# Attention of the first network: heads in pairs on the two halves of the TensorE array, the mask added in PSUM, another spread of the convolution's taps

## The reference

```python
h = modulate(rmsnorm(x, norm1_g[l]), sh1, sc1)
p = h @ w_in[l]                      # GLU 2x512 | q k v 3x512 | two gates 2x1024
q = rope_2d(q, ...); k = rope_2d(k, ...)
y_conv = conv_branch(...)            # GLU, depthwise convolution of 31 taps, layernorm, silu, @ w_conv_out
# neighbourhood attention, 8 heads of 64; all 4 grid rows, a window of 16 of 64 columns, and the context
s_win = einsum("bhqd,bhiqjd->bhqij", q_r, k_win) * scale + rpb[...]
s_ctx = einsum("bhqd,bhcd->bhqc", q_r, k_ctx) * scale
p = softmax(concatenate([s_win, s_ctx]))
y = p_win @ v_win + p_ctx @ v_ctx
# first layer only: the context attends to itself, with softmax(q_c k_c * scale) v_c
x = x + g1 * ((sigmoid(p_gate) * [y_conv, y_attn @ w_na_out]) @ w_out)
x = x + g2 * conv_ffn(modulate(rmsnorm(x), sh2, sc2))
```

## Time and profile before

| | us |
|---|---|
| median of 3 runs (2118.94 to 2122.93) | 2121.02 |
| the profiled execution | 2119.22 |
| its span, first to last instruction | 2117.4 |

### The profile page before, as it was taken

One profiled execution on the slowest core, in us unless ns is written; L12 is line 12 of the kernel. 1 busy time (PEld: TensorE's weight loads), 2 busy tenths in 40 slices (PEclk: granted clock), 3 DMA queues, 4 the chain that ended last, 5 costly groups with the idle time before them and its releaser, 6 DMA issues.

```text
span 2117.4 us, 34274 instructions
## 1 busy us (share of the span) xinstructions
PE 2014.3 (95%) x12568; PEld 1697.1 (80%) x12568; DVE 1022.9 (48%) x1916; ACT 889.8 (42%) x1505; POOL 1185.1 (56%) x904
## 2 busy tenths in 40 slices
PE   5999999999999999999999999899899999989997
PEld 3666666777888788887789998787799987769997
DVE  3167876726343322587666732466542034546402
ACT  3222433424333322525546644446454343545533
POOL 1332333343544555454487986564588856629885
PEclk8999999999999999999999999999899999989999
DMA  9799221233623232344344575333355544315663
GB/s 390 273 343 326 65 60 60 75 117 75 162 89 99 90 100 89 95 125 115 95 160 142 186 222 171 108 112 102 95 177 179 178 141 153 109 59 180 185 185 107
DMA packets 115686, 306.55 MB, mean 145 GB/s; under 512 B 29672, under 2 KB 44392, under 8 KB 115316
## 3 DMA queue, kind: packets, MB, share of 16 engines
q1 hardware_dynamic: 112664, 298.06, 43.9%
q10 hardware_dynamic: 2908, 6.90, 1.7%
HBM read 300.19 MB, written 8.06 MB: 146 GB/s over the span
## 4 chain that ended last, share of the span: by engine, by line
issue 42%; POOL 37%; PE 18%; DVE 1%; POOLq 0%; ACT 0%; DMA 0%; ACTq 0%
POOL w_lo L600 37%; PE bank L1082 5%; PE bank L1084 4%; PE bank L1083 4%; PE bank L1483 1%; PE bank L1484 1%; PE bank L1485 1%; DVE nb L1725 0%; PE bank L1659 0%; DVE u_lo L1733 0%; PE bank L1512 0%; POOLq L596 0%; PE bank L1699 0%; PE bank L1675 0%; PE bank L1605 0%
## 5 line engine op out<-in xcount | busy, mean ns | idle before, releaser
L600 POOL TENSOR_TENSOR w_lo<-raw,w_hi 128x512 fp32r<-128x512 f32 x884 | 1167.5, 1346 | 911.1 <-ACT w_hi L641 910.6
L641 ACT ACTIVATE w_hi<-raw 128x1024 fp32r<-128x1024 f32 x442 | 466.3, 1056 | 321.2 <-PE bank L1084 250.4
L1082 PE MATMUL bank<-h_hi,w_hi 128*128 128x512 f32 (+1 forms) x1216 | 423.4, 348 | 8.2 <-POOL w_lo L600 4.3
L1083 PE MATMUL bank<-h_lo,w_hi 128*128 128x512 f32 (+1 forms) x1216 | 415.3, 341 | 0.0
L1084 PE MATMUL bank<-h_hi,w_lo 128*128 128x512 f32 (+1 forms) x1216 | 415.2, 341 | 0.0
L1082 PEld LDWEIGHTS bank<-h_hi,w_hi 128*128 128x128 f32 x1216 | 229.0, 188 | 64.8 <-issue 27.6
L1082 PE MATMUL bank<-u_hi,w_hi 128*128 128x272 f32 (+1 forms) x880 | 255.0, 290 | 9.5 <-POOL w_lo L600 4.2
L1084 PEld LDWEIGHTS bank<-h_hi,w_lo 128*128 128x128 f32 x1216 | 229.1, 188 | 29.3
L1083 PEld LDWEIGHTS bank<-h_lo,w_hi 128*128 128x128 f32 x1216 | 229.2, 188 | 28.2 <-issue 0.2
L1083 PE MATMUL bank<-u_lo,w_hi 128*128 128x272 f32 (+1 forms) x880 | 251.7, 286 | 0.0
L1084 PE MATMUL bank<-u_hi,w_lo 128*128 128x272 f32 (+1 forms) x880 | 251.5, 286 | 0.0
(11 more groups left out here) (289 smaller groups left out, 3494.0 us busy)
## 6 DMA issues: line engine op xcount, KB each, us to landing
raw<-in_wstream SPq DMA_DIRECT2D x442, 512.0 KB, 3.6
ada_raw<-in_wada SPq DMA_DIRECT2D x96, 512.0 KB, 7.0
biash<-rpb_by_offset SPq DMA_DIRECT2D x64, 64.0 KB, 3.5
rpb_by_offset<-in_rpb SPq DMA_DIRECT2D x16, 224.0 KB
bias_by_distance<-vec ACTq DMA_DIRECT2D x1, 3264.0 KB
bias<-bias_by_distance SPq DMA_DIRECT2D x2, 1632.0 KB, 8.7
X<-in_x_in ACTq DMA_DIRECT2D x1, 2048.0 KB, 11.9
bias<-bias_by_distance SPq DMA_DIRECT2D x2, 864.0 KB, 6.7
```

The source lines that it names most:

```text
L600: i = pool.tensor_tensor(w_lo[:, s, part], raw[:, s, part], w_hi[:, s, part].bitcast(F32), ALU.subtract)
L641: act.activation(w_hi[:, s, :], raw[:, s, :], ACT.Copy).then_inc(sem("w_hi_ready"), 1)
L1082: pe.matmul(o, hi, a_hi, start=start, stop=False)
L1083: pe.matmul(o, hi, a_lo, start=False, stop=False)
```

## The change

- Heads are handled as pairs (2p, 2p+1). `scores_x` takes a list of heads: for pairs 1 to 3 the scores of both heads are issued together, half t=0 of both and then t=1 of both; heads 0 and 1 stay apart.
- `values` takes a pair: for each block of keys the even head's product and then the odd one's, into the two column halves of bank 7; `pt_x` and `pt_c` exist twice. Rounding and rest of the values are made once for a pair, on 128 partitions.
- `turn` becomes `turn_x` and `turn_c`, separate steps; the context scores of the even head follow the pair's scores, those of the odd head its transposes.
- The mask is no longer added to the bias: for each half it is added to the scores in PSUM behind the bias.
- VectorE walks a list of its own, `VECTOR1_PLAN`, with the taps as steps: in the first layer 3, 7 and 4 in a pair, 6 beside each v slab; in the second 2, 5 and 3, and 10.
- Bias loads of heads 2 and up stand one (even) or two (odd) slabs earlier on the queue.

```diff
-        pt_x = at("pt_x", [4, 256], F32, work + 6144)
-        pt_c = at("pt_c", [2, 256], F32, work + 10240)
+        pt_x = [at(f"pt_x{u}", [4, 256], F32, o) for u, o in enumerate((work + 6144, nb_at))]
+        pt_c = [at(f"pt_c{u}", [2, 256], F32, o) for u, o in enumerate((work + 10240, nb_at + 4096))]
...
+            V_ = [("V", p - 1)] * (p > 0)
+            if p:
+                L1_PLAN += [("Sx", e, o), ("Sc", e), ("gate", 4 * p)] + V_
+            else:
+                L1_PLAN += [("gate", 0), ("Sx", o)]
+            L1_PLAN += [("gate", 4 * p + 1), ("Tx", e), ("Tc", e), ("gate", 4 * p + 2), ("Tx", o), ("Sc", o)]
+            L1_PLAN += [("mean", 0)] * last + [("gate", 4 * p + 3), ("Tc", o)]
+            VECTOR1_PLAN += [("Sx", e, o), ("Sc", e)] if p else [("Sx", o)]
+            VECTOR1_PLAN += [("tap", 2), ("Tx", e), ("Tc", e)] + V_
+            VECTOR1_PLAN += [("tap", 5 if not last else 0), ("Tx", o), ("Sc", o), ("tap", 3 if not last else 0)]
+            VECTOR1_PLAN += [("mean", 0)] * last + [("Tc", o)]
...
-        TAPS_QK, TAPS_V, TAPS_HEAD = 7, 4, 4
+        TAPS_QK, TAPS_V = 7, (6, 10)
...
-                    loads(gate + 2 * h + 2)
+                    loads(gate + 2 * h + (1, 0)[h % 2])
...
+            def scores_x(layer, heads):
                 pe.wait_ge(*after("rope_out", (layer, 2 * QC - 1)))
                 for t in range(2):
+                    for h in heads:
+                        claim(sx_bank(h, t))
+                for t in range(2):
+                    for h in heads:
+                        r = slice((h % 2) * HD, (h % 2) * HD + HD)
+                        b = sx_bank(h, t)
+                        pe.matmul(bank[b][:, :], qT[r, h // 2, t * P:(t + 1) * P], kT[r, h // 2, :], start=True, stop=True)\
+                            .then_inc(*done("attn_score", (layer, h, t)))
...
+            def values(layer, p):
                 claim(7)
...
                 for k in range(4):
...
+                    for u in range(2):
+                        h = 2 * p + u
+                        mm = pe.matmul(aux[3][u * HD:(u + 1) * HD, 0:SEQ], V[:, k, h * HD:(h + 1) * HD], pt_x[u][:, k, :],
+                                       start=k == 0, stop=k == 3)
...
                     if 0 in units:
                         dve.wait_ge(*after(f"bias_in{h % 2}", (layer, h, 1, 1)))
-
-                        m = win.unsqueeze(1).to_broadcast((P, 8, GRID_W))
-                        tt(bh.rearrange("p t (a b) -> p (t a) b", a=4), bh.rearrange("p t (a b) -> p (t a) b", a=4), m, ALU.add)\
-                            .then_inc(*done("bias_masked", (layer, h)))
-                        dve.wait_ge(*after("bias_masked", (layer, h)))
+                    window = win.unsqueeze(1).to_broadcast((P, 4, GRID_W))
...
                             tt(ps[:, 0:SEQ], ps[:, 0:SEQ], bh[:, u, :], ALU.add).then_inc(*done("attn_added", (layer, h, u)))
+                            near = ps[:, 0:SEQ].rearrange("p (a b) -> p a b", a=4)
                             dve.wait_ge(*after("attn_added", (layer, h, u)))
+                            tt(near, near, window, ALU.add).then_inc(*done("attn_windowed", (layer, h, u)))
+                            dve.wait_ge(*after("attn_windowed", (layer, h, u)))
...
+                    elif kind == "tap":
+                        tap(h * (3 - layer) // 2 if h else len(taps))
```

More of the change, by code:

```diff
@@ L313, in parts @@
             return [(s, slice(s * SEQ, (s + 1) * SEQ)) for s in range(2 if layer == 0 else 1)]
[L318 to L323, removed]
-        TAPS_QK, TAPS_V, TAPS_HEAD = 7, 4, 4
+        L1_PLAN, VECTOR1_PLAN = [], []
+        for p in range(HEADS // 2):
+            e, o = 2 * p, 2 * p + 1
+            last = o == HEADS - 1
+            V_ = [("V", p - 1)] * (p > 0)
[9 more added lines that the diff above has]
+            VECTOR1_PLAN += [("mean", 0)] * last + [("Tc", o)]
+        L1_PLAN += [("V", HEADS // 2 - 1), ("var", 0)]
+        VECTOR1_PLAN.append(("V", HEADS // 2 - 1))
+        TAPS_QK, TAPS_V = 7, (6, 10)
         def sx_bank(h, t):
@@ L730, in attend @@
                     elif kind == "Sx":
[L731 to L735, removed]
+                        for n in (n,) + others:
+                            for t in range(2):
+                                act.wait_ge(*after("attn_max", (layer, n, t)))
+                                m = 4 * (n % 2) + t
+                                act.activation(px(n)[:, t, :], bank[sx_bank(n, t)][:, :], ACT.Exp, bias=small[:, m:m + 1],
+                                               accum_out=small[:, 8 + m:9 + m]).then_inc(*done("attn_exp", (layer, n, t)))
                     elif kind == "Sc" and layer == 0:
@@ L1244, in network1 @@
                     elif kind == "Sx":
[L1245 removed]
+                        scores_x(layer, step[1:])
                     elif kind == "Sc":
                         scores_c(layer, n)
[L1248 to L1249 removed]
+                    elif kind == "Tx":
+                        turn_x(layer, n)
+                    elif kind == "Tc" and layer == 0:
+                        turn_c(layer, n)
                     elif kind == "V":
@@ L1436, in values, with turn_c @@
-            def values(layer, h):
-                r = slice((h % 2) * HD, (h % 2) * HD + HD)
+            def turn_c(layer, h):
+                pe.wait_ge(*after("attn_prob", (layer, h, 3)))
+                for t in range(2):
+                    for k in range(2):
+                        mm = pe.transpose(aux[2][:, (2 * t + k) * P:(2 * t + k + 1) * P], p_c[:, t, k * P:(k + 1) * P], ident)
+                mm.then_inc(*done("attn_turned", (layer, h, 2)))
+                readers[6] = ("attn_pt", (layer, h, 2))
@@ L1438, in values @@
+            def values(layer, p):
                 claim(7)
                 pe.wait_ge(*after("v_out", (layer, 3)))
-                pe.wait_ge(*after("attn_pt", (layer, h, 2 if layer == 0 else 1)))
+                for h in (2 * p, 2 * p + 1):
+                    pe.wait_ge(*after("attn_pt", (layer, h, 1)))
+                    if layer == 0:
+                        pe.wait_ge(*after("attn_pt", (layer, h, 2)))
                 for k in range(4):
-                    mm = pe.matmul(aux[3][r, 0:SEQ], V[:, k, h * HD:(h + 1) * HD], pt_x[:, k, :],
-                                   start=k == 0, stop=k == 3)
@@ L1893, in biased_max, with probabilities @@
                         dve.tensor_reduce(small[:, m:m + 1], x, AXX, ALU.max, negate=True).then_inc(*done("attn_max", (layer, h, u)))
-                def probabilities(h):
-                    for u in [0, 1] + [2, 3] * (layer == 0):
+                def probabilities(h, units):
+                    for u in units:
                         m = 16 + 4 * (h % 2) + u
```

95 lines of the change are left out of this document (41 added, 54 removed).

## The result

| | before | after |
|---|---|---|
| median of 4 runs each, us | 2121.44 | 2093.82 (2093.33 to 2095.26) |
| ratio | | 0.9872, 95% interval 0.9855 to 0.9889 |
| the profiled execution | 2119.22 | 2095.26 |
| its span | 2117.4 | 2093.5 |

The change takes 27.6 us off the median; forecast were 2092 and a gain of 28.8. Between the two profiled executions it is 24.0, since that of before lay 2.2 under its median and that of after was the slowest of its four. The steps of the forecast are held against those 24.0.

A forecast was written before the change was run, and what follows sets the result against it. TensorE's own instructions were taken to set the pace, with VectorE 20% free. 18.4 + 11.5 + 5.2 = 35.1 us off TensorE, less 6.3 of new waits, gave 28.8 and a median of 2092, range 2085 to 2106.

The forecast's parts named there:

- Value products, 18.4: Values of two heads in alternating column halves cost what one head did; 4 blocks go in each layer, 18.4 us.
- scores, 11.5: Scores of three pairs a layer overlap in the two row halves; 3 blocks of 1.91 go in each layer, 11.5 us.
- the reserve of 4 us: Possible loss in the value pairs, 0.05 us a round; taken as 0, with 4 us kept for the range.
- The wait behind the context copy, 5.2: TensorE's 7 waits for ScalarE's copy of turned context probabilities, 6.0 us, go; one of 0.85 returns, gain 5.2.
- Mask, loads, copies, 0: Mask additions moved to PSUM, earlier bias loads and ScalarE's copies; loads and copies priced at 0, mask delay in waits.
- New waits, 6.3: TensorE waiting for VectorE, mainly at transposes: 3.1 us in the first layer and 3.2 in the second, given back.
- The later ones: First layer: head 1's context turn 0.2, later pairs 0.15 x 2; second layer: head 1 0.1, two later pairs 1.2.
- VectorE as the bound: Rival: GpSimd's traffic stretches the mask additions in PSUM from 0.42 to 0.9; 2101, at worst 2106; chance 0.13.
- No new waits: Rival: VectorE is always in time, so nothing is given back; 2086; chance 0.10.
- Weight loads in the open: Rival: value-pair matmuls overlap, but 80 rounds each show two loads of 0.14, 22 us; 2114; chance 0.02.
- no overlap: Rival: the array halves don't overlap, so 29.9 us of gain are gone; 2116; chance 0.03.
- slower: Rival: value and score halves don't overlap and it ends on the slow side from 0.025 us a record; chance 0.02.

The follow-up runs named there:

- the first three expectations: Changed kernel issued head by head: scores expected 2101 to 2104, measured 2094.76; values 2109 to 2111, measured 2101.90; both 2118 to 2121, measured 2100.54.
- experiments 1 to 3: Changed kernel: scores, values or both head by head (0.9874, 0.9923, 0.9905); also a whole-array product between or ahead of heads (1.0048, 0.9958); values in short runs (2093.2 us).
- the taps placed anew: Changed kernel with the 124 taps moved, fewer ahead of the probabilities and more behind the last context turn: 2084.09 us, ratio 0.9828.

## Why the prediction was right, and where it was not

- *Value products, 18.4, and scores, 11.5.* The blocks came out as forecast (2.74, 1.88, 1.82, 1.91), none of the reserve of 4 us was needed. TensorE's busy time fell by 16.25 and 11.67 in the two attentions, 27.9 in place of 29.9. Of the missing 2, 1.5 lie in the second layer, and 1.4 of them would be the 0.28 booked as busy at its five new waits (an estimate from the one wait measured above). The outcome was right, the reason taken for it, here and in the first three expectations, was not: the alternation of records isn't what makes the halves overlap. Neighbourhood in the queue is, up to four records (experiments 1 to 3). Alternation is worth about 7 us for values and nothing for scores.
- *The wait behind the context copy, 5.2.* 6.0 became 0.83.
- *Mask, loads, copies, 0.* Right for the mask as far as the runs tell, not contradicted for the loads. The unit of 1.54 was forecast as 1.55.
- *New waits, 6.3.* This is the step that failed in size. The first turns of each layer and V were forecast at 4.5 (1.1 + 1.5 + 0.7 + 1.2) and measured 4.4 (0.32 + 0.76 + 0.27, 1.5, 0.6 more for V, 0.96). (The 0.7 for V is 0.6 by the prediction's own numbers, 2.4 less 1.76.) The later ones, "0.15 x 2", "0.6, in two pairs", 0.1 and 0.2, sum to 1.8 and measured 4.9: seven waits of 0.47 to 0.75. The three context turns were put at 0.5 and cost 2.2, head 1 of the second layer was put at 0.1 and cost 1.2, the two pairs behind it were put at 1.2 and cost 1.5. The term took one probability at 0.59 from the earlier trace rows, where it ran free of GpSimd; its multiplication is 0.49 of that, and beside `w_lo` it takes up to 1.3. For the two later pairs the near hit is luck: VectorE's path was forecast to end at 14.3, it ended at 14.9, and at 13.9 without GpSimd's share, when there was no wait. The taps were taken at 1.0, a price that did hold GpSimd's share; they ran at 0.77 in the place shown above, and in the mean from 190 to 352 at 0.89, before at 1.04. The stretch had changed its place, from taps and mask additions that nobody waits for to the instruction that TensorE waits for.
- *Sum, in the profiled executions.* 27.9 + 5.2 - (5.1 + 4.3) = 23.7, and the two stretches are 23.8 shorter. Forecast 28.8: 2.0 are missing in busy time and 3.1 in the waits. The median came nearer (2093.8 to 2092) because the gap between the medians is 3.7 wider than that between the profiled executions; that is luck, not foresight.
- *The rivals.* VectorE as the bound was right in its cause, GpSimd's traffic, and wrong in the victim, the additions in PSUM. No new waits is what the taps placed anew nearly reach. Weight loads in the open, no overlap and slower didn't happen, but the last two are real elsewhere: with a whole-array product between the heads the kernel is slower than before.

## What to carry to other kernels

Two small matmuls in different halves of the array ran together when they stood close in TensorE's queue and no product of the whole array stood between; here up to four records were looked past. Before pricing an instruction that an engine's order will move, look at what GpSimd did while it was timed: a price of 0.49 taken in a quiet stretch became 1.3 beside it here. And a wait inside a stream of matmuls cost its recorded length of 0.75 and 0.28 more.

## What the runs showed of the hardware

- A matmul of one column half started before matmuls of the other half that precede it in the program (256.49 before 256.70), and blocks of two heads in three different orders have the lengths that a lookahead of four records (two products) gives (3.65, 4.51 and 2.35 us).
- A product of 128 x 8 columns over the whole array costs 0.22 us ahead of such a block (252.90 to 253.12) and 0.32 in the midst of it (257.26 to 257.58).
- With GpSimd's subtractions cut to a sixteenth the whole kernel took 2052.6 us (one execution), 41 less than the changed one: 6.8 in the first attention, 3.7 in the second, 3.8 between them, 28 behind them. TensorE's 13.7 us of waits for `w_lo` are gone, which is a third; the rest I didn't follow.
